# Eleven weight-rest subtractions of a first layer's input projection, moved from VectorE to GpSimd

## What is computed

```python
def conformer_conv(u, w_dw, b_dw, ln_g, ln_b):
    a, g = jnp.split(u, 2, axis=-1)
    y = a * jax.nn.sigmoid(g)
    y = lax.conv_general_dilated(y, w_dw[:, None, :].astype(y.dtype), ...) + b_dw   # depthwise, 31 taps
    return jax.nn.silu(layernorm(y, ln_g, ln_b))

q, k, v, u = jnp.split(h_lat @ w_in, cuts, axis=-1)
...
q = apply_rope(rmsnorm(split_heads(q, N_HEADS), q_g), cos, sin)
k = apply_rope(rmsnorm(split_heads(k, N_KV_HEADS), k_g), cos, sin)
...
o_lat = jnp.concatenate([a_lat, c_lat], axis=-1) @ w_out
```

## Time and profile before

| | us |
|---|---|
| median of three runs | 1497.35 |
| lowest and highest | 1496.7, 1498.34 |
| the profiled execution | 1495.29 |
| its span, first to last instruction | 1493.5 |
| granted TensorE clock, mean | 0.977 |

### The profile page before, as it was taken

How to read it: one execution, slowest core, us unless ns; L and a number is a source line. 1 busy time by engine, 2 the same in 40 slices (tenths; PEclk the granted TensorE clock), 3 DMA queues, 4 the chain that set the end, 5 groups by cost and what they waited for, 6 DMA issues and landing times.

```text
span 1493.5 us, 25370 instructions
## 1 busy us (share of the span) xinstructions
PE 1385.8 (93%) x11135; PEld 822.5 (55%) x11135; DVE 525.5 (35%) x954; ACT 398.7 (27%) x701; POOL 4.1 (0%) x8
## 2 busy tenths in 40 slices
PE   6899889999999999989798999999999997799865
PEld 3688558888888888878584343333332332233221
DVE  2799885422232333579953102011100001001112
ACT  3522484522222222475562101010110000001001
POOL 0000000000000000000000000000000000000010
PEclk9899999999999999999999999999999999999998
DMA  9997903533231142510526899999999999999995
GB/s 351 385 337 276 347 1 113 170 113 100 70 113 57 43 182 86 189 41 25 197 113 261 320 400 406 409 408 407 409 406 409 406 409 408 408 409 402 409 407 202
DMA packets 147029, 395.89 MB, mean 265 GB/s; under 512 B 7488, under 2 KB 38752, under 8 KB 146912
## 3 DMA queue, kind: packets, MB, share of 16 engines
q1 hardware_dynamic: 144000, 388.86, 68.5%
q10 hardware_dynamic: 2336, 3.24, 0.6%
q0 software_dynamic: 576, 2.10, 0.4%
HBM read 390.76 MB, written 3.41 MB: 264 GB/s over the span
## 4 chain that ended last, share of the span: by engine, by line
PE 73%; DMA 13%; DVE 6%; SPq 6%; ACT 1%; issue 1%; DVEq 0%; ACTq 0%
PE bank L1187 20%; DMA weight_ring<-in_exp_w 10%; PE bank L1145 7%; PE bank L1012 5%; PE bank L1011 5%; PE bank L1010 5%; SPq L575 4%; PE bank L733 4%; PE bank L734 4%; PE bank L735 3%; PE bank L1019 3%; PE bank L1021 3%; PE bank L1020 3%; PE bank L679 2%; PE bank L1153 2%; DMA weight_ring<-in_w_ada 2%
## 5 line engine op out<-in xcount | busy, mean ns | idle before, releaser
L1187 PE MATMUL bank<-weight_ring,gathered 128*32 128x512 f32 (+1 forms) x3840 | 397.7, 565 | 33.0 <-DMA weight_ring<-in_exp_w 33.0
L1187 PEld LDWEIGHTS bank<-weight_ring,gathered 128*32 128x32 f32 x3840 | 125.9, 111 | 282.1 <-issue 281.1
L2226 DVE TENSOR_TENSOR scratch<-scratch,bank 64x512 f32<-64x512 f32 (+1 forms) x60 | 38.4, 639 | 399.8 <-ACT scratch L1646 397.2
L1145 PE MATMUL bank<-weight_ring,scratch 128*32 128x512 f32 x1360 | 162.4, 598 | 9.0 <-DMA weight_ring<-in_exp_w 8.8
L1012 PE MATMUL bank<-slot_halves,slot_halves 128*128 128x512 f32 x336 | 130.9, 390 | 0.0
L1011 PE MATMUL bank<-hT_halves,slot_halves 128*128 128x512 f32 x336 | 130.9, 390 | 0.0
L1010 PE MATMUL bank<-slot_halves 128*128 128x512 f32 x320 | 124.7, 390 | 0.0
L734 PE MATMUL bank<-hT_halves,slot_halves 128*128 128x512 f32 (+1 forms) x352 | 122.2, 347 | 0.0
L1832 DVE SCALAR_TENSOR_TENSOR weight_ring<-scratch,conv_weights,weight_ring 128x512 f32<-128x512 f32 (+1 forms) x207 | 121.3, 637 | 2.6 <-ACT weight_ring L1427 0.7
L733 PE MATMUL bank<-slot_halves,slot_halves 128*128 128x512 f32 (+1 forms) x284 | 106.0, 373 | 8.6 <-DVE slot_halves L1739 5.7
L1145 PEld LDWEIGHTS bank<-weight_ring,scratch 128*32 128x32 f32 x1360 | 43.7, 111 | 112.1 <-issue 91.5
(11 more groups left out here) (301 smaller groups left out, 1576.0 us busy)
## 6 DMA issues: line engine op xcount, KB each, us to landing
weight_ring<-in_exp_w SPq DMA_DIRECT2D x216, 1024.0 KB, 18.3
weight_ring<-in_w_ada SPq DMA_DIRECT2D x24, 2048.0 KB, 14.0
weight_ring<-in_exp_w SPq DMA_DIRECT2D x64, 768.0 KB, 15.6
weight_ring<-in_ffn_w SPq DMA_DIRECT2D x33, 1024.0 KB, 5.5
weight_ring<-in_w_in SPq DMA_DIRECT2D x8, 1024.0 KB, 11.6
weight_ring<-in_w_out SPq DMA_DIRECT2D x4, 2048.0 KB, 11.5
weight_ring<-in_w_in SPq DMA_DIRECT2D x2, 3072.0 KB, 15.4
expert_rows<-scratch ACTq DMA_DIRECT2D x14, 128.0 KB, 6.0
```

The lines of the kernel that those rows point to most:

```text
L1145: i = mm(bank[6][quarter, :], at01[:, c0:c0 + BLOCK], w2[:, i_, half * 512:(half + 1) * 512], start=(first and i_ == 0), stop=(last and i_ ...
L1187: i = mm(ps[BLOCK * job:BLOCK * (job + 1), 0:cw], gathered_block(e, k, b), w[:, kk, a * cw:(a + 1) * cw], start=(k == 0), stop=(k == KT - 1))
```

## The change

The eleven rests of tiles 3 to 13 of the first layer leave VectorE's queue, from between its taps and from steps 0 to 2, and become eleven `tensor_tensor` subtractions at the head of GpSimd's queue. GpSimd first waits for the three rests that VectorE still makes (tiles 0 to 2), since `mx_lo` counts in order, and then for each head. The operands, the results, the semaphores and the waits of TensorE are the same. The order and number of the taps on VectorE are the same.

```diff
@@ -1254,6 +1254,12 @@
                     pool.indirect_dma_start(chosen[i], None, rows_kept[:, :],
                                             bass.IndirectOffsetOnAxis(ap=row_at[:, i:i + 1], axis=0)
                                             ).then_inc(row_back, 16)
+
+            pool.wait_ge(mx_lo, 3)
+            for i in range(3, IN_TILES):
+                pool.wait_ge(mx_hi, i + 1)
+                pool.tensor_tensor(mixer_tile(i, True), mixer_tile(i), mixer_hi(i).bitcast(F32),
+                                   ALU.subtract).then_inc(mx_lo, 1)
 
             rounds(pool, rows_fetched, lambda r, last: None)
 
@@ -1842,11 +1848,9 @@
                 for c in range(NC):
                     gated_unit(c)
                     if l == 0:
-                        mixer_rest(0, 2 * c + 3)
                         conv_steps(TAPS_AT_UNIT[c][0])
                         if c == 3:
                             modulation(0, 1)
-                        mixer_rest(0, 2 * c + 4)
                         conv_steps(TAPS_AT_UNIT[c][1])
                     elif c == 1:
                         for i in range(4):
@@ -1879,8 +1883,6 @@
 
                 dve.wait_ge(rest_in, 16)
                 for st in range(6):
-                    if l == 0 and st < 3:
-                        mixer_rest(0, V_TILE + 3 + st)
                     at = st - 1
                     if at == 0:
                         dve.wait_ge(m["root"], 2)
```

## The result

| | before | changed |
|---|---|---|
| median, us | 1497.82 (4 runs) | 1504.14 (4 runs) |
| lowest and highest | 1496.7, 1498.34 | 1503.47, 1506.0 |
| profiled execution, and its span | 1495.29, 1493.5 | 1503.97, 1502.2 |

The changed kernel takes 1.0044 times as long, with an interval of 1.003 to 1.0057: slower by 6.3 us, between 4.5 and 8.5. The forecast was 1504.9, slower. The sign, the place and the size came out, but the size in good part by luck: three terms of the sum were off and a fourth was missing, and the errors nearly cancel.

What follows compares the result with a forecast made beforehand. TensorE was taken as the bound, VectorE close behind. Eleven holds of 2.28 us (25.1) less 17.6 for work removed, idle time, slack and a weights wait gave +7.5 us on 1497.35: 1504.9 us, range 1496.5 to 1510.

Steps and rivals of the forecast that it cites:

- the instruction with the least slack: The key's normalisation on VectorE (L1895), ending at 139.09, 0.2 us before TensorE's rotation (L799) needs it.
- the rests themselves come in time: GpSimd's rests would be ready before TensorE wants their tiles; the tightest, tile 9, has 4.5 us left.
- nothing behind 166 us gives the lag back: Attention and dense layer are paced by TensorE, and the expert weights are asked for after its second projection.
- The term h: Length of one GpSimd subtraction, taken as 2.28 us (1.14 to 3.4), all of it lost by VectorE, eleven times.
- rival C: In between: VectorE loses 1.1 to 1.87 us per subtraction, at most +3.0 us; chance 0.06.
- The slack: VectorE's idle times between 58.1 and 138.4 us, ahead of L1895, would absorb 3.4 us of the hold.
- the forecast's step for this wait: TensorE reaches the rotation (L799) later by 11h - 16.1, with h = 2.28 us.
- The credit of 1.5 us: TensorE's 1.54 us wait for weights at 163.12 would shrink as TensorE comes later, giving that time back.
- B, side by side: GpSimd's subtractions cost VectorE nothing, so the time stays at 1497.4 us; chance 0.34.
- D, starvation: GpSimd gets in only when a burst of VectorE's taps ends, so rests come late: near +15 us, 1512; chance 0.10.
- E: Faster, only if the shorter VectorE queue removes a wait that the trace doesn't list; chance 0.03.

Runs made afterwards that it cites:

- the memset: Kernel before with added GpSimd memsets of 1024 columns (no input, one output), all rests still on VectorE: 1497.44 us, 0.9996.
- run 5: Changed kernel with the rests of tiles 3 to 8 back on VectorE, only those of tiles 9 to 13 on GpSimd: 1500.67 us, 1.0021.
- run 6: First half of the output projection's weights asked for later in SyncE's list: 1496.8 us on the kernel before, 1505.12 us on the changed one.
- run 3: Changed kernel with 24 added matmuls (results unused) on TensorE before the rotation that waits for the key's normalisation: 1501.14 us, 1.0023.
- run 1: Kernel before, all rests on VectorE, with added GpSimd subtractions (ten released by heads of tiles 3 to 12, three near 235 us): 1514.61 us, 1.011.

## Why the prediction was right, and where not

*Right.* What bounds the kernel (TensorE, with VectorE close behind); that the work taken away could gain nothing; the instruction with the least slack and its 0.2 us; that the rests themselves come in time; that VectorE is held for most of each subtraction; and that nothing behind 166 us gives the lag back. Of the hold the Trainium skill's "SBUF — State Buffer", section "Who interferes with whom", said: a VectorE instruction with two SBUF inputs and a GpSimd one that reads SBUF exclude each other, and one that GpSimd only writes does not. Taps of 2.77 us, the unhurt PSUM product of 0.68 us and the memset's 749 ns agree with that. The Trainium skill's sentence there, that whoever issues first has the shared ports for the whole instruction, doesn't say how long the other can be kept out; run 5 shows a GpSimd subtraction at 8.98 us among taps.

*The term h* was mis-sized. I took 2.28 us for what VectorE loses to each of eleven, 25.1 us in all; the steps of VectorE give 20.5, 1.86 each, and no single hold over 2.15. The operation itself is a little longer than I took it for, 2.4 us, and the hold is shorter than the operation. By the prediction's own sum the measured holds make 20.5 - 17.6 = +2.9 us, which is inside its 0.2% and on the ground of its rival C. That the time still came out at the forecast has three other reasons.

*The slack* was counted too high. Not every idle time ahead of L1895 could be used: at the first tap, where the kernel before has 0.43 us of idle time behind a rest, the changed one has 1.90, because the tap waits for ScalarE, whatever VectorE has been relieved of. L1897 came 5.6 us later, counted from TensorE's L828. So of the 20.5 - 12.5 = 8.0 us of net hold only 2.4 went into idle time, not 3.4. With the 0.2 us of slack this leaves 5.4, and TensorE's wait is 5.35; the forecast's step for this wait was 9.0.

*The credit of 1.5 us* at the wait for weights failed. It gave 0.2: a gap inside the piece took its place (run 6). The gap isn't bound to come, since run 3 has the full credit.

*The clock* was missing from the sum altogether, +2.9 us. I worked out the length of an idle stretch of TensorE and did not ask what TensorE does behind it. Run 3 shows that the term is real: with TensorE busy in that stretch, tile 12 takes 2.8 us less.

So the sum was 9.0 - 1.5 = 7.5, and the trace has 5.4 + 2.9 - 0.2 = 8.0 to the scores. The hold was 4.6 us too large, and 1.0 of slack, 2.9 of clock and 1.3 of credit were missing, which makes up for it; that is luck. The medians differ by 6.3, in an interval of 4.5 to 8.5 that holds both. The profiled executions differ by 8.7, but the one of before is 2.5 under its median. Between the two traces the lag is still 7.8 us at 489 us and 8.0 near 1459, so in this pair of executions nothing gives it back.

*The rivals.* B, side by side, is refuted by the taps of 2.77 and 2.89 us beside GpSimd, and by run 1. C had the right size of the mean hold, just inside its 1.87 us, but not the time: its bound of +3.0 went by the same slack and credit, and without the clock. D, starvation, happens in single instructions and never reached TensorE. E had nothing: no run was faster than before beyond its interval.

## What to carry to other kernels

GpSimd is no free engine for reading work while VectorE is busy: ask what VectorE executes in those microseconds, and count the hold (2.0 to 2.1 us for 1024 columns with two inputs, beside taps) against what was taken away (1.14 us). Then follow the holds to the one instruction behind them that another engine waits for; moving eight taps past it was, within the scatter of the runs, worth as much as undoing the whole change. And when a sum ends in a wait of TensorE, price its clock after the wait too: 5.4 us of idling cost 2.9 us more.

## What the runs showed that I had not expected

- A TensorE that idled for 5.35 us ran at 1.2 GHz up to 150 us, some 5.6 us; useless matmuls in the gap kept the clock at 2.4 GHz and took 2.8 us off the tile behind it.
- A GpSimd copy (1.08 us alone) costs VectorE 0.53 us on the mean and 0.78 beside taps, a subtraction (2.4 alone) 2.0 to 2.1 beside taps, a memset (0.99 alone) nothing.
- GpSimd can be kept out: 8.98 us for a subtraction of 2.4, beside taps that follow one another closely.
- VectorE's one-input scalings out of SBUF are held as well (one for 2.1 us), and so are instructions of two columns (one for 1.4 us).
- A gap of 0.5 to 1.0 us behind the 36th matmul of one modulation piece, absent where a wait for weights or 24 more matmuls stand ahead of it.
